# Two transformer blocks in one kernel: the row-maximum products of each attention's first pair moved ahead of its loop

## What is computed

```python
proj = h @ w_in
cq, ckv, k_rope, fq, fk, fv, f_logit, g_mla, g_fox = jnp.split(proj, IN_OFFSETS, axis=-1)
...
o_mla = causal_block_attention(q_mla, k_mla, v_mla, MLA_SCALE)
...
o_fox = causal_block_attention(fq, fk, fv, FOX_SCALE, f_cum)
y = sigmoid(g_mla) * (o_mla @ w_o_mla) + sigmoid(g_fox) * (o_fox @ w_o_fox)
return y @ w_out

# causal_block_attention, per block of queries
logits = einsum('bqhd,bkhd->bhqk', qi, k) * scale     # FoX adds F[t] - F[s], a running sum of log forget gates
logits = where(mask, logits, -inf)
p = softmax(logits)
return einsum('bhqk,bkhd->bqhd', p, v)
```

## Time and profile before

| | us |
|---|---|
| median of 3 runs | 3068.46 |
| lowest, highest | 3067.79, 3071.77 |
| profiled execution | 3067.74 |
| its span, first to last instruction | 3065.9 |
| busy: TensorE, VectorE, GpSimd, ScalarE | 2945.7, 1593.8, 1072.9, 788.4 |
| FoX's products and loop | about 1738 to 1903 |
| MLA's products and loop | about 1950 to 2152 |

### The profile page before, as it was taken

How to read it: one execution, slowest core, us unless ns; L and a number is a source line. 1 busy time by engine, 2 the same in 40 slices (tenths; PEclk the granted TensorE clock), 3 DMA queues, 4 the chain that set the end, 5 groups by cost and what they waited for, 6 DMA issues and landing times.

```text
span 3065.9 us, 34100 instructions
## 1 busy us (share of the span) xinstructions
PE 2945.7 (96%) x13230; PEld 2343.0 (76%) x13230; DVE 1593.8 (52%) x1566; ACT 788.4 (26%) x1054; POOL 1072.9 (35%) x474
## 2 busy tenths in 40 slices
PE   6999998899999999889999999999999999999998
PEld 5876676688888888667888866766887888888886
DVE  3629954735655565784342065555546333343356
ACT  2128952412222121332002133234013111111112
POOL 2330024244444444343444430410444333333342
PEclk9999999999999999999999989999999999999999
DMA  2120032012222221131313344421421111111112
GB/s 109 48 76 21 9 123 83 31 61 102 94 103 90 103 96 69 62 118 63 117 62 125 117 92 127 107 49 40 153 89 42 48 48 48 48 48 48 48 49 75
DMA packets 85010, 233.02 MB, mean 76 GB/s; under 512 B 19312, under 2 KB 27760, under 8 KB 84144
## 3 DMA queue, kind: packets, MB, share of 16 engines
q1 hardware_dynamic: 79616, 211.49, 21.0%
q10 hardware_dynamic: 5296, 20.19, 1.6%
HBM read 176.26 MB, written 28.05 MB: 67 GB/s over the span
## 4 chain that ended last, share of the span: by engine, by line
PE 73%; issue 8%; DVE 8%; ACT 1%; POOL 1%; SPq 0%; DMA 0%; DVEq 0%; POOLq 0%; ACTq 0%
PE ps L364 55%; PE ps L418 4%; PE ps L1242 3%; PE ps L2365 2%; PE ps L2338 2%; PE ps L2042 1%; PE ps L2379 1%; DVE stick_sp L992 1%; PE ps L2755 1%; DVE stick_sp_hi L1003 1%; DVE stick_a L1016 1%; POOL w_hi L316 1%; POOL w_lo L319 1%; DVE residual L1362 1%; PE ps L3244 1%
## 5 line engine op out<-in xcount | busy, mean ns | idle before, releaser
L316 POOL TENSOR_TENSOR w_hi<-w_raw,inv_count 128x1024 fp32r<-128x1024 f32 x186 | 356.7, 1917 | 1560.1 <-PE ps L364 988.5
L319 POOL TENSOR_TENSOR w_lo<-w_raw,w_hi 128x1024 fp32r<-128x1024 f32 x186 | 495.8, 2666 | 14.6
L364 PE MATMUL ps<-x_hi,w_hi 128*128 128x512 f32 x1104 | 342.6, 392 | 6.1 <-DVE qkvu_raw L841 4.8
L364 PE MATMUL ps<-x_lo,w_hi 128*128 128x512 f32 x1104 | 340.9, 390 | 0.0
L364 PE MATMUL ps<-x_hi,w_lo 128*128 128x512 f32 x1104 | 340.8, 390 | 0.0
L364 PEld LDWEIGHTS ps<-x_hi,w_hi 128*128 128x128 f32 x1104 | 207.8, 189 | 52.0 <-issue 6.5
L364 PE MATMUL ps<-hidden_hi,w_lo 128*128 128x512 f32 x800 | 246.3, 389 | 0.0
L364 PE MATMUL ps<-hidden_lo,w_hi 128*128 128x512 f32 x800 | 246.3, 389 | 0.0
L364 PE MATMUL ps<-hidden_hi,w_hi 128*128 128x512 f32 x800 | 246.3, 389 | 0.0
L364 PEld LDWEIGHTS ps<-x_lo,w_hi 128*128 128x128 f32 x1104 | 207.9, 188 | 43.5
L364 PEld LDWEIGHTS ps<-x_hi,w_lo 128*128 128x128 f32 x1104 | 207.8, 188 | 43.4
(11 more groups left out here) (442 smaller groups left out, 5272.1 us busy)
## 6 DMA issues: line engine op xcount, KB each, us to landing
w_raw<-wall SPq DMA_DIRECT2D x217, 512.0 KB, 3.2
ada_raw<-wada SPq DMA_DIRECT2D x48, 512.0 KB, 4.2
gates_scratch<-gate_out ACTq DMA_DIRECT2D x16, 512.0 KB, 2.6
gate_in<-gates_scratch SPq DMA_DIRECT2D x8, 1024.0 KB, 7.5
residual<-x_t SPq DMA_DIRECT2D x8, 512.0 KB, 8.9
residual<-x_t SPq DMA_DIRECT2D x2, 2048.0 KB, 9.5
emb_scratch<-emb_out ACTq DMA_DIRECT2D x8, 512.0 KB, 2.6
embedding<-emb_scratch SPq DMA_DIRECT2D x4, 1024.0 KB, 6.5
```

Of the source, the lines that this page charges most:

```text
L316: nc.gpsimd.tensor_tensor(w_hi[:, slot, :], w_raw[:, slot, :], one.to_broadcast([P, S]), ALU.mult).then_inc(w_split, 1)
L319: nc.gpsimd.tensor_tensor(w_lo[:, slot, :], w_raw[:, slot, :], w_hi[:, slot, :].bitcast(F32), ALU.subtract).then_inc(w_split, 1)
L364: last = nc.tensor.matmul(ps[:, banks + c, :], lhs, x[:, k0 + k, c * HALF:(c + 1) * HALF], start=k == 0 and n == 0, stop=k == nk - 1 and n ...
```

## The change

- FoX: all 12 products of pair 0 and row product 0 stand ahead of the loop, among the last parts of gate 15: products 2 and 3 before its third part, row product 0 and product 4 before the fifth, 5 and 6 before the sixth, 7 and 8 before the seventh, 9, 10 and 11 before the eighth. ScalarE copies unit 0's rows before gate 15's sigmoid.
- MLA: row product 0 and product 4 are issued behind the last query tile, from the function of that stage; products 5 to 11 follow ahead of the loop.
- Later pairs, in both attentions: steps 5 to 8 issue one product of the next pair, steps 9 to 11 two, the next pair's steps 0 and 1 one each, step 2 none.

```diff
@@ in2_scalar
-        for g in range(8, N_GATES):
+        for g in range(8, N_GATES - 1):
             gate(g)
+        with after(IN2):
+            fox.row_copy(act, 0)
+        gate(N_GATES - 1)
         load_exp_ln()
@@ in2_tensor
-        product(pe, b % 2, 0, 8, x_hi, x_lo, 0, 6, range(4))
-        with after(IN2):
-            fox.largest(pe, 2)
-            fox.largest(pe, 3)
-        product(pe, b % 2, 0, 8, x_hi, x_lo, 0, 6, range(4, 8)).then_inc(w_used, 1)
+        product(pe, b % 2, 0, 8, x_hi, x_lo, 0, 6, range(2))
+        for k, ms in ((2, (2, 3)), (3, ()), (4, (4,)), (5, (5, 6)), (6, (7, 8)), (7, (9, 10, 11))):
+            with after(IN2):
+                for m in ms:
+                    if m == 4:
+                        fox.rows(pe, 0)
+                    fox.largest(pe, m)
+            last = product(pe, b % 2, 0, 8, x_hi, x_lo, 0, 6, range(k, k + 1))
+        last.then_inc(w_used, 1)
@@ maxes_to
         if s < 0:
-            return 6
+            return 12
         p, r = divmod(s, 12)
-        own = 8 + 2 * min(r, 2)
-        return min(12 * p + own + max(0, r - 4), len(MAXES))
+        own = 12 if p == 0 else min(11 + r, 12)
+        return min(12 * p + own + max(0, r - 4) + max(0, r - 8), len(MAXES))
@@ Attention.tensor
-            for m in range(done, 4):
-                self.largest(pe, m)
-            self.rows(pe, 0)
-            for m in range(4, maxes_to(-1)):
+            for m in range(done, maxes_to(-1)):
                 self.largest(pe, m)
@@ Attention.scalar (row_copy becomes a method; the first copy is left out where rows_done is 1)
-            row_copy(0)
+            if not rows_done:
+                self.row_copy(act, 0)
@@ fox_scalar, fox_tensor, mla_scalar, mla_tensor
-        fox.scalar(act, also)
+        fox.scalar(act, also, 1)
-        fox.tensor(pe, 4)
+        fox.tensor(pe, 12)
-        mla.scalar(act, also)
+        mla.scalar(act, also, 0)
-        mla.tensor(pe, 4)
+        mla.tensor(pe, 5)
@@ proj_tensor (q_block also calls between(2) behind its last tile)
-        q_block(3, lambda step: largest(2, 3) if step else largest(1))
+        def last_between(step):
+            if step == 2:
+                with after(PROJ):
+                    mla.rows(pe, 0)
+            largest(*((1,), (2, 3), (4,))[step])
+        q_block(3, last_between)
```

More of the change, by code:

```diff
@@ L2409, in tensor, with row_copy, scalar @@
                     sums(u)
[L2411 to L2417, removed]
+        def row_copy(self, act, u):
+            act.wait_ge(*row_full.at(u + 1))
+            for h in range(2):
+                r = 32 + 64 * h
+                nc.scalar.activation(self.row_out(u // 2, h)[:, (u % 2) * HALF:(u % 2 + 1) * HALF],
+                                     ps[r:r + 4, self.bank("row", u), :], ACT.Copy).then_inc(row_done.sem, 1)
+        def scalar(self, act, also, rows_done):
             def exp(k):
@@ L2434, in inverse @@
                 nc.scalar.activation(self.inv[:, :], self.inv[:, :], ACT.Exp, scale=-1.0).then_inc(inv_done.sem, 1)
-            row_copy(0)
+            if not rows_done:
+                self.row_copy(act, 0)
             for s in range(NA + 3):
                 for u in rows_due(s):
-                    row_copy(u)
+                    self.row_copy(act, u)
                 if s < NA:
@@ L2766, in q_block @@
             q_tile(n + 1, b % 2, 3, range(1, 3)).then_inc(w_used, 1)
+            between(2)
         def largest(*ms):
```

## The result

| | before | after |
|---|---|---|
| median, us (4 runs each) | 3070.11 | 3093.07 |
| lowest to highest | 3067.79 to 3072.86 | 3092.46 to 3095.26 |
| profiled execution; its span | 3067.74; 3065.9 | 3092.46; 3090.7 |
| mean granted clock | 0.983 | 0.979 |

The kernel before has one run more here than in the table ahead of the prediction. The ratio is 1.0075 (95% interval 1.0061 to 1.0089). The median of 3093.07 compares with a forecast of 3075.4 and a range of 3068 to 3083; the span grew by 24.8 us, where 6.9 were forecast.

The account below looks back on a forecast made before the run. TensorE, busy 96% of the span, was taken as the bound, so gains could only come from its idle time or clock. FoX +4.6 and MLA +2.3 gave +6.9 us, a median of 3075.4, range 3068 to 3083.

Parts of the forecast that it names:

- FoX, pair 0: First attention's start: stalls go, but product 12 waits some 15 us, starting 2.5 later; half clock behind it adds 4.5.
- rival 2: FoX stays at half clock behind product 12 as long as before: +12 in place of 4.5, 3083 us; chance 0.16.
- the chain, unchanged in length: FoX: GpSimd's operations and SP's moves for pair 1's operands still take 24.0 us, starting 7.9 later, ending at 1784.8.
- FoX, later pairs: FoX after pair 0: the twelfth product comes a step sooner, so the negation is ready: -2.4 us.
- MLA, pair 0: Second attention's start: product 12 starts 0.9 later after a wait of about 4.7; half clock adds 2.2: +3.1 us.
- VectorE's q_rope_low takes 1.22: MLA, pair 1's query split: duration in us taken for this operation, ending it at 1980.9 before eight transfers.
- MLA, the turns: MLA's later pairs: -1.0 us towards pair 2 (ends -3.9 and +0.7), +0.9 in pair 3's turn (0 to 3).
- The last pair: MLA's last pair: has no successor and only loses its 0.7 us stall: -0.7.
- the four: The rivals: clock soon back in FoX and MLA (3071.8 us, chance 0.26), rival 2, Rival 3 and rival 4.
- signs named for a right forecast: Gate 15 ending near 1761, FoX's some 15 us wait, MLA waits of 2 to 5, hardly any for the negation.
- Rival 3: FoX's product 12 isn't held: the 7.0 us fall away and 13 are won, 3055 us; chance 0.05.
- rival 4: VectorE becomes the bound in double steps: 0.5 to 1 us in each of six turns, 3079 us; chance 0.05.

Follow-up runs that it names:

- e3: Changed kernel, but GpSimd splits the keys of MLA's pairs 2 and 3 only after VectorE has split the previous pair's queries; 3089.82 us.
- e5: Changed kernel with MLA's queries split sooner and pair 1's query transfers ahead of its key transfers, TensorE's order kept; 3067.31 us.
- e6: Changed kernel with FoX's products 4 to 11 behind gate 15's last part and MLA's order of before; 3069.47 us.
- e1: Changed kernel with FoX as changed and MLA's order of before; 3077.11 us.
- e4: Kernel before, but GpSimd splits the keys of MLA's pairs 2 and 3 only after VectorE's split of the previous pair's queries; 3068.42 us.
- e8: Kernel before with only MLA's later pairs as changed, MLA's pair 0 and all of FoX as before; 3080.08 us.
- e12: e11 with no product in step 10 of FoX's pair 0, three in steps 11 and 12 and two in step 13; 3048.88 us.
- e11: Changed kernel with FoX's products 4 to 11 behind gate 15, pair 1's from step 8, and MLA's queries split early; 3050.09 us.
- e9: Changed kernel with FoX's products 4 to 11 behind gate 15, pair 1's from step 8, and MLA's order of before; 3064.22 us.

## Why the prediction was wrong, point by point

**FoX, pair 0: the mechanism right, its sizes nearly.** GpSimd's first memset started at 1759.81 (put: gate 15's end near 1760.8), product 12 at 1784.69 (put: 1784.8) behind a wait of 15.9 us (put: some 15), with half clock for 9 us behind it and 4.5 lost, as put. That 4.5 is partly luck: in e3 and e5 the half clock behind the same wait lost 8.0, midway to rival 2's 12. Against FoX's own first product it is held by 3.3 us, not 2.5: "the chain, unchanged in length" was 0.9 longer, since GpSimd's four splits took 9.6 us (1.99, 2.98, 2.22, 2.40) beside VectorE's additions and 8.6 where e6 runs them (1.90, 2.38, 1.90, 2.39). e6 shows that the chain starts at gate 15's end.

**FoX, later pairs: -2.4 put.** Those waits went, but a new one of 0.6 for a bank and slips of under 1 us each took most of it back: from product 12 to the next stage it took 3.5 us more than before, 4.5 of which is clock. So FoX came to +6.9 for +4.6.

**MLA, pair 0: the steps that failed.** First, the length of VectorE's split. "VectorE's q_rope_low takes 1.22" was read where GpSimd was idle. It took 3.36, and the copy before it 1.99; q_rope_low ended at 1990.36 instead of 1986.8 (the 1980.9 of the text and the 5.9 by which MLA began later). Up to there the forecast was exact: q_rope_high ended at 1985.6, as put. Product 12 started 8.7 us behind q_rope_low, for a landing put at 7.8. Product 12 was held by 5.2 us (43.3 less 38.1) for 0.9. In e3, without the collision, q_rope_low ends where it was put, 31.1 us behind MLA's first product, TensorE waits 4.9 (put: 4.7) and the hold is 1.7. Second, the price of the half clock: it lost 4.9 for 2.2, and 5.3 even in e3, after a wait of the length foreseen, so this term was too small without any collision.

The rule of the Trainium skill (SBUF — State Buffer, Who interferes with whom) that a VectorE instruction with two SBUF inputs contends with a GpSimd instruction that reads SBUF was weighed for the turn from pair 1 to pair 2 alone, and set aside. The trace agrees with it, in pair 0 too: q_rope_low has two SBUF inputs and took 3.36 us beside the key split, 1.22 in e3; it ended 1.1 us behind GpSimd's second split (1989.27), nearly its own length, as if it had waited for the whole of that one. In the turn it was weighed for, q_low took 3.35 us. The copy (1.99) and the negation's first instruction (1.90 in e1) were held with one tensor input, so this rule alone doesn't cover all that was held.

**MLA, the turns: -1.0 and +0.9 put.** From product 12 to 24 it took 6.5 us more than before, of which 4.9 are the half clock counted above; the other 1.6 stand against -1.0, past the upper end of +0.7. From the first scores to product 24 it took 22.7 us for the 16.9 put: q_rope_low ended 13.5 us behind these scores instead of 9.1, and product 24 started 9.3 behind that instead of 7.8. VectorE's instructions were held again, by the key split and by the weight splits behind it, now in front of the last reduction and the negation:

```profile
2036.17 3.35 DVE L2647 TENSOR_TENSOR mla_q_low<-mla_q,mla_q_high 128x1024 fp32r<-128x1024 f32 x1
2039.45 1.98 DVE L2484 COPY mla_p_sum<-mla_p 128x256 f32<-128x256 f32 x1
2041.35 1.21 DVE L2460 TENSOR_REDUCE stat<-ps 128x1 f32<-128x1024 f32 x1
2042.59 1.14 DVE L2467 TENSOR_SCALAR mla_neg_max<-stat 128x8 fp32r<-128x8 f32 x1
...
2036.05 2.39 POOL L2911 TENSOR_TENSOR mla_k_low<-mla_k,mla_k_high 128x1024 fp32r<-128x1024 f32 x1
2038.41 2.87 POOL L316 TENSOR_TENSOR w_hi<-w_raw,inv_count 128x1024 fp32r<-128x1024 f32 x1
```

So the 2.8 us stall and its half clock, which the forecast had as gone, came back as 3.3 us with 2.6 lost behind it. From product 24 to 36 it took 5.0 us more, 3.4 of them half clock behind product 24's wait; without these the 1.6 is inside the bounds of 0 to 3. The last pair brought 0.8 more instead of 0.7 less, with 1.7 at half clock. So MLA came to +17.6 for +2.3.

What share has each step? Without the collision (e3) MLA is 6.1 us shorter, and still 9 above the forecast. The larger part is clock: MLA's busy time rose by 8.0 us with the same matmuls, where the forecast took 1.7 and 2.9 of half clock away, put 2.2 in pair 0 and left the turns' half clock to their bounds.

**The rivals.** None of the four was it. The case that happened is the forecast's mechanism with nearly all of MLA's terms past their upper ends together; that they share one cause, the late queries, e5 shows. Of the signs named for a right forecast FoX gave all; MLA's first wait (8.4 for 2 to 5) and its 3.3 us at the row product were against it. Rival 3 (not held) is excluded by e6 and the 15.9 us; rival 4 (VectorE the bound) shows in the changed kernel only as a wait of 0.6 us.

**The root.** What limits this change in MLA is that a pair's queries are split behind the exponentials of steps 0 and 1, while the change puts less of TensorE's work between the first scores and the next pair's first product. e5 shows it: with the split moved, and with it pair 1's query transfers put ahead of its key transfers, 28.7 us came back in the same order of TensorE. Which of the two did more isn't tested. In FoX it is that moving work ahead of gate 15's end delays the start of a chain that was not on the path before: by e6 this is some 7.5 of the 15.9 us, and the rest is that TensorE, freed of its stalls, comes sooner than the chain ends.

## What to carry to other kernels

Before moving work ahead on the bounding engine, list what starts behind the place that it is moved to (a semaphore, an exponential with other work hung on it) and how much slack that chain has; move the start of the chain first. Where TensorE waits at a repeated place, price the half clock behind each wait together with the wait, and in every later turn. A duration read where a neighbour engine was idle is a lower bound once the phases shift.

## What the hardware showed that was not expected

**The clock behind waits of like length differs.** TensorE waited 2.16 us in front of MLA's row product 1 before the change and in e4. Before, 1982 to 1986 us was then granted 0.57; in e4 the clock stayed full:

```profile
1980.00:1986.00 6.00, 5.69 (x31) 4.01 (x32) 1.25 (x4) 2.40 (x4) 4.93 (x2) 1.00 0.99 237
```

Behind the wait of 2.47 us at product 36 the changed kernel lost 1.7 us; behind one of 2.47 at the same product e8 lost 11.17 × 0.43 = 4.8:

```profile
2087.00:2099.00 12.00, 11.17 (x39) 7.65 (x40) 3.38 (x4) 2.25 (x3) 0.00 (x0) 0.57 0.00 0
```

Behind waits of 1.7, 2.1 and 2.6 us (e12, e11, e9) some 3.4, 6.8 and 6.8 us were lost, more than the waits themselves, and behind the same 15.9 us wait 4.5 in one execution and 8.0 in another.

**An eight-column VectorE instruction can stand still for the length of a GpSimd one.** An instruction of the negation took 1.90 us in e1, beside a key split of 1.89, and 1.07 and 1.81 in e4, beside a key split and a weight split, for 0.17 each; taking a collision off one instruction put it on another.
